# Attention scores of a two-branch streaming encoder: chunk mask written into PSUM by VectorE, score blocks joined and issued in one piece

## The chip, the cores and the metric

One core of one Trainium2 chip runs the whole program. The metric is the device time of one execution in microseconds; the time of a kernel is the median of its runs.

## The reference

Two layers of an encoder work on 320 tokens: 256 of a prompt and 64 of a second request (the sample), whose 256 earlier keys and values lie in a cache. Model width is 1024, everything is fp32. In a layer, one wide projection of the normed input feeds two branches, an attention branch and a gated linear attention (GLA) branch; the branches are projected, gated and merged, then a feed-forward layer and a per-layer input gate follow.

The change touches the attention branch alone. It has 8 heads; each head has two softmax maps (m = 0, 1) of 64 channels, and subtracts the second, times lambda, from the first:

```python
def diff_attend(q, k, v, lam, mask):
    s = jnp.einsum('bqhmd,bkhmd->bhmqk', q, k) * (A_DH ** -0.5)
    if mask is not None:
        s = jnp.where(mask, s, -jnp.inf)
    p = jax.nn.softmax(s, axis=-1)
    a = p[:, :, 0] - lam * p[:, :, 1]
    return jnp.einsum('bhqk,bkhe->bqhe', a, v)
...
        mask = k_chunk[None, :] <= q_chunk[:, None]
```

The mask is block-causal over chunks of 64 prompt tokens: a query sees the keys of its own chunk and of all earlier chunks. The sample attends to its cached and its own 64 keys without a mask.

## The kernel before

**Layout and stages.** Activations lie transposed in SBUF, 128 channels on the partitions and the 320 tokens along the free axis. Every projection is cut into tiles of 128 output channels. A tile is computed in 8 chunks of 128 input channels (k = 0 to 7), each with three matmuls, because weights and inputs are split into a high and a low part: lines 1201, 1202 and 1203 in `tile`. Its result grows in one of two PSUM banks, `big[0]` and `big[1]`. Weights come in by DMA (SP's queue, `w_raw`), ScalarE makes their high part (L559, `w_hi`), VectorE the low part (L843, `w_lo`), and PE waits for it at the head of a tile.

**The mix loop.** In each layer, the wide projection is run in 4 iterations of 16 tiles (`MIX_IT`, `MIX_N`), so that there are eight iterations in all. An iteration makes two attention heads and one GLA head. Its tiles are, in order: GLA queries and keys (0, 1), attention keys (2, 3), queries (4, 5), GLA values (6, 7), attention values (8, 9), and gates (10 to 15). The small matmuls of the two branches are issued by hand between the tiles or, through the generator argument `between` of `tile`, between the chunks of a tile: after each chunk, `tile` takes one step of the generator (L1206). Each engine has its own hand-written order of the same loop, and semaphores join them.

**The scores.** `scores(0)` (head 0 of the iteration) is stepped in tile 7 and `scores(1)` in tile 11. Its first two steps issue nothing. The third, after chunk k = 2, waits for the rotary result and the copied keys (head 0) or for the copied attention maps of head 0 (head 1), and issues the first matmuls. The scores go to PSUM: `X[4]` for map 0 and `X[5]` for map 1, with columns 0 to 255 for the second block of 128 queries (all 256 keys) and columns 256 to 383 for the first block (128 keys); `X[0]` for the sample (256 cached keys, then 64 own). For each block of queries:

- L1284: the keys that all queries of the block see (192 or 64 columns), one matmul per map; then a yield, so a chunk of the tile comes next;
- L1288: the last 64 keys, one matmul per map, left open for accumulation;
- L1290: one matmul per map with a contraction of one row, which adds -1e30 to the scores of the block's first 64 queries with these keys (`mq`, a row of the constants); then a yield.

The sample's scores (L1297, cached keys, a yield, own keys) close the piece, and the last one raises `scores_done`. In this way a head's scores spread over the chunks k = 2 to 7 of its tile. An fp32 matmul is shown as two records in the trace, an accumulating one of the tiles (fp32r) as one.

**What follows the scores.** On VectorE, `negmax` (L953) waits for `scores_done`, takes five row maxima (L956, L957, L958) and scales them (L960). In program order it stands in step t = 7 (head 0) and t = 11 (head 1), behind the weight split of that step and ahead of the copy of that tile's result. ScalarE's `exps` (L655) then makes the exponentials and, behind them, the next weight splits. VectorE's `difference` (L965 to L974) follows in step 8 (head 0) or 12 (head 1); behind head 0's stand the masked sums of the GLA branch (L1040, L1043). PE transposes the maps in `att_transposes` (L1305 to L1309) after tile 9 (head 0) and tile 13 (head 1). After tile 9 it first waits for the first masked sum (L1395), then transposes the GLA values (L1211).

**What stands behind tile 7 on PE.** After tile 7, PE waits for the decayed GLA queries and keys (`gla_qk_ready`), which VectorE makes in step t = 6 (L1021 to L1028, from `E`), transposes the keys (L1211) and multiplies pairs (L1392). After tile 11 come the GLA's own sums (L1328).

**Counting.** `Steps` counts the VectorE instructions of an iteration that raise `dve_mix` (19 before), so that a wait on all of them so far can be put anywhere.

Of the kernel before, what the change touches and what calls it, by code (L numbers as in the profile page):

```python
# [26 lines left out]
P = 128  # L27
# [6 lines left out]
HEADS, DH, DV = 8, 64, 128  # L34
GH, GDK, GDV, RANK = 4, 128, 256, 16
CH = 64
# [36 lines left out]
K_ID, K_ONE, K_EPS = 0, 128, 256  # L73
# [8 lines left out]
K_MQ = K_ID2 + 64  # L82
# [26 lines left out]
def snap(eng, value):  # L109

    return value if isinstance(value, int) else eng.snap(value)
# [19 lines left out]
def encoder(nc, A, O):  # L131
# [27 lines left out]
    def sb(name, shape, dt=F32, where=ctx):  # L159
        return where.enter_context(nc.sbuf_tensor(name, shape, dt))  # L160

    def sem(name):
        return ctx.enter_context(nc.semaphore(name))
# [8 lines left out]
    cst = sb("cst", [P, NCONST])  # L172
# [86 lines left out]
    X = [ctx.enter_context(nc.psum_tensor(f"X{i}", [P, 512], F32)) for i in range(6)]  # L259
# [111 lines left out]
    dve_pro, dve_mix = sem("dve_pro"), sem("dve_mix")  # L371
# [460 lines left out]
    def _(dve):  # L832
# [46 lines left out]
        for l in range(DEPTH):  # L879
# [36 lines left out]
            for j in range(MIX_IT):  # L916
                tb = snap(dve, l * TILES + j * MIX_N)
                rb = snap(dve, l * RESULTS + j * MIX_N)
                v = snap(dve, l * MIX_IT + j + 1)
                st = Steps(dve, dve_mix, v * 19 - 19, 19)  # L920

                def at(per, k):
                    return v * per + (k - per)
# [28 lines left out]

                def negmax(h):  # L953
                    dve.wait_ge(scores_done, at(2, h + 1))
                    for m in range(2):
                        nc.vector.tensor_reduce(mx[:, m:m + 1], X[4 + m][:, 2 * P:3 * P], AX.X, ALU.max)  # L956
                        nc.vector.tensor_reduce(mx[:, 2 + m:3 + m], X[4 + m][:, 0:2 * P], AX.X, ALU.max)  # L957
                    st.put(nc.vector.tensor_reduce(mx[:, 4:5], X[0][:, 0:PAST + TS], AX.X, ALU.max))  # L958
                    st.wait()
                    nc.vector.tensor_scalar(nb[:, :], mx[:, :], -DH ** -0.5, None, ALU.mult).then_inc(negmax_ready, 1)  # L960
# [20 lines left out]
                for t in range(MIX_N):  # L981
# [32 lines left out]
                    if t in (6, 7):  # L1014
                        if t == 7:
                            negmax(0)
                        out_tile(vgT[:, t - 6, :], t)
# [28 lines left out]
                    if t in (10, 11):  # L1046
                        if t == 10:
                            dve.wait_ge(vg_trans, 2 * v)
                        else:
                            negmax(1)  # L1050
                        out_tile(zr[:, t - 10, :], t)
# [57 lines left out]
            for j in range(OUT_IT):  # L1109
                tb = snap(dve, l * TILES + j * OUT_N + OUT_0)  # L1110
                for t in range(OUT_N):
                    lo(tb, t + 2, KC)
                    dve.wait_ge(tile_done, tb + (t + 1 + CREDIT_TILE))
                    m = j * 4 + t
# [26 lines left out]
            for j in range(FDN_IT):  # L1141
                tb = snap(dve, l * TILES + j * FDN_N + FDN_0)
                for t in range(FDN_N):
                    lo(tb, t + 2, FDN_K[(t + 2) // 2 % 3])
                    if t // 2 % 3 == 2:
                        dve.wait_ge(tile_done, tb + (t + 1 + CREDIT_TILE))
                        m = j * 4 + t // 6 * 2 + t % 2
# [7 lines left out]
            for j in range(PLE_IT):  # L1155
                tb = snap(dve, l * TILES + j * PLE_N + PLE_0)
                n8 = snap(dve, l * KC + j * PLE_N)
                for t in range(PLE_N):
# [9 lines left out]
                    m = j * 4 + t  # L1168
# [17 lines left out]
    def _(pe):  # L1186
        mm = nc.tensor.matmul
# [50 lines left out]
        for l in range(DEPTH):  # L1238
# [17 lines left out]
            for j in range(MIX_IT):  # L1256
                tb = snap(pe, l * TILES + j * MIX_N)
                rb = snap(pe, l * RESULTS + j * MIX_N)
                v = snap(pe, l * MIX_IT + j + 1)
                xc = snap(pe, l * 24)  # L1260

                def at(per, k):
                    return v * per + (k - per)

                def scores(h):


                    q, k, kc = qr[:, h, :], kr[:, h, :], kcT[:, h, :]
                    mq = cst[0:1, K_MQ:K_MQ + P]
                    yield  # L1270
                    yield
                    if h == 0:
                        pe.wait_ge(rope_ready, 2 * v)
                        pe.wait_ge(k_copied, at(7, 5))
                    else:
                        pe.wait_ge(att_copied, at(6, 3))

                    for at0, q0, nk in ((0, P, 2 * P), (2 * P, 0, P)):
                        for m in range(2):
                            r = slice(m * DH, (m + 1) * DH)
                            mm(X[4 + m][:, at0:at0 + nk - CH], q[r, q0:q0 + P], k[r, 0:nk - CH], start=True, stop=True)  # L1284
                        yield
                        for m in range(2):
                            r = slice(m * DH, (m + 1) * DH)
                            mm(X[4 + m][:, at0 + nk - CH:at0 + nk], q[r, q0:q0 + P], k[r, nk - CH:nk], start=True, stop=False)  # L1288
                        for m in range(2):
                            mm(X[4 + m][:, at0 + nk - CH:at0 + nk], mq, cst[0:1, K_ONE:K_ONE + CH], start=False, stop=True)  # L1290
                        yield
                    for at0, keys in ((0, kc), (PAST, k[:, TP:T])):
                        if at0:
                            yield
                        for m in range(2):
                            r = slice(m * DH, (m + 1) * DH)
                            last = mm(X[0][r, at0:at0 + (PAST if at0 == 0 else TS)], q[r, TP:T], keys[r, :], start=True, stop=True)  # L1297
                    last.then_inc(scores_done, 1)
# [54 lines left out]
                for t in range(MIX_N):  # L1353
                    pe.wait_ge(result_read, rb + (t - 1 + CREDIT_RES))
                    tile(tb, t, x_hi, x_lo, chunk_wait=(xlo_ready, xc) if t == 0 else None,
                         between={7: scores(0), 11: scores(1), 15: gla_outputs()}.get(t, ()))
                    if j == t == 0:
                        if l:
# [114 lines left out]
            with pe.Fori(0, FDN_IT) as j:  # L1473
                tb = snap(pe, l * TILES + j * FDN_N + FDN_0)
                for t in range(FDN_N):
                    pair, k, mt = t // 6, t // 2 % 3, t % 2
# [39 lines left out]
        for c in range(KC):  # L1516
            pe.wait_ge(y_ready, c + 1)
            half, m = c // 4, c % 4
# [81 lines left out]
```

## Time and profile before

| What | Value |
|---|---|
| Time, median of 3 runs | 1573.46 us (1572.07 to 1576.39) |
| The profiled execution's own time | 1574.4 us |
| Its span, first to last instruction | 1572.6 us |
| PE (TensorE matmul) busy | 1520.7 us, 97% of the span |
| PEld (its weight loads, beside PE) | 1418.0 us, 90% |
| DVE (VectorE) busy | 872.0 us, 55% |
| ACT (ScalarE) busy | 622.8 us, 40% |
| POOL (GpSimd) busy | 243.3 us, 15% |
| HBM traffic | 121 GB/s over the span |
| Mean granted TensorE clock | 0.956 of 2.4 GHz |

How to read it: busy times are the union of an engine's instructions. Matmuls are pipelined, so one lasts longer in the record than the distance to the next; what a piece of PE work costs is read from start to start. The eight iterations of the mix loop lie in 30 to 430 us and 800 to 1200 us of the span. An idle stretch of an engine is written in brackets behind the instruction that ends it, with what it waited for. The granted clock is 1.00 at 2.4 GHz and 0.50 at 1.2 GHz; the value of a window is its mean.

### The profile page before, as it was taken

How to read it: one execution, taken by the hardware profiler on the slowest of the kernel's cores; microseconds unless marked ns; L12 is line 12 of the kernel's file. 1: busy time of each engine (PE TensorE's matmuls, PEld its weight loads, DVE VectorE, ACT ScalarE, POOL GpSimd, SP SyncE). 2: the span in 40 equal slices, each digit the busy share in tenths (PEclk: the TensorE clock that was granted, in tenths of full speed). 3: DMA queues.
4: the chain of work that ended last, by engine and by line, in shares of the span. 5: the costliest groups of instructions: out<-in, count | busy, mean ns of one | idle time of the engine just before them, and what ended most of it. 6: DMA issues, size and time to landing. Idle time of an engine off the chain costs nothing.

```text
span 1572.6 us, 25415 instructions
## 1 busy us (share of the span) xinstructions
PE 1520.7 (97%) x10019; PEld 1418.0 (90%) x10019; DVE 872.0 (55%) x1408; ACT 622.8 (40%) x1037; POOL 243.3 (15%) x276
## 2 busy tenths in 40 slices
PE   6899999999999999999989999999999999999997
PEld 4789888898799999999978898988888999999997
DVE  4653636546466655545556366463654565555546
ACT  3343343433463444333343244343345443343343
POOL 0302103021002200012422030110300050000224
PEclk9998989989899999999989799898997999999999
DMA  6467855555234444444423665335431445444443
GB/s 157 109 86 90 108 111 124 80 112 108 81 120 150 147 147 150 152 155 139 143 85 111 111 99 89 95 114 114 110 113 62 152 134 160 149 145 153 156 141 101
DMA packets 195552, 191.29 MB, mean 122 GB/s; under 512 B 9126, under 2 KB 192236, under 8 KB 195468
## 3 DMA queue, kind: packets, MB, share of 16 engines
q1 hardware_dynamic: 192352, 181.76, 46.1%
q0 software_dynamic: 2688, 7.35, 1.2%
q8 instruction: 57, 0.93, 0.2%
q10 hardware_dynamic: 428, 1.03, 0.2%
q14 instruction: 27, 0.22, 0.0%
HBM read 181.45 MB, written 8.65 MB: 121 GB/s over the span
## 4 chain that ended last, share of the span: by engine, by line
PE 85%; POOL 5%; DVE 5%; DMA 2%; ACT 2%; issue 1%; ACTq 0%; DVEq 0%; SPq 0%; POOLq 0%
PE big L1201 24%; PE big L1202 21%; PE big L1203 21%; PE X L1346 2%; POOL E L527 2%; DMA w_raw<-in_w_in 2%; PE X L1392 2%; PE X L1345 2%; PE X L1328 1%; POOL E L528 1%; PE X L1290 1%; DVE w_lo L843 1%; PE X L1211 1%; POOL rot L534 1%; PE X L1297 1%
## 5 line engine op out<-in xcount | busy, mean ns | idle before, releaser
L1201 PE MATMUL big<-x_hi,w_hi 128*128 128x320 f32 x1984 | 656.8, 331 | 20.4 <-DVE x_lo L1092 6.9
L1202 PE MATMUL big<-x_lo,w_hi 128*128 128x320 f32 x1984 | 625.3, 315 | 0.0
L1203 PE MATMUL big<-x_hi,w_lo 128*128 128x320 f32 x1984 | 624.2, 315 | 0.0
L843 DVE TENSOR_TENSOR w_lo<-w_raw,w_hi 128x1024 fp32r<-128x1024 f32 (+1 forms) x330 | 418.6, 1271 | 109.9 <-ACT w_hi L559 109.5
L1201 PEld LDWEIGHTS big<-x_hi,w_hi 128*128 128x128 f32 x1984 | 382.7, 193 | 56.6 <-issue 38.1
L1202 PEld LDWEIGHTS big<-x_lo,w_hi 128*128 128x128 f32 x1984 | 384.6, 194 | 3.5 <-issue 1.6
L559 ACT CAST w_hi<-w_raw 128x1024 fp32r<-128x1024 f32 x328 | 331.1, 1038 | 142.5 <-PE big L1203 86.3
L1203 PEld LDWEIGHTS big<-x_hi,w_lo 128*128 128x128 f32 x1984 | 383.7, 193 | 0.0
L504 POOL TENSOR_TENSOR sqt<-xT 128x320 f32<-128x320 f32 x47 | 48.0, 1021 | 637.3 <-DVE xT L1149 422.6
L1201 PE MATMUL big<-h_hi,w_hi 128*128 128x320 f32 x352 | 109.1, 310 | 0.0
L1203 PE MATMUL big<-h_hi,w_lo 128*128 128x320 f32 x352 | 108.9, 309 | 0.0
L1202 PE MATMUL big<-h_lo,w_hi 128*128 128x320 f32 x352 | 108.9, 309 | 0.0
L655 ACT ACTIVATE p<-X,nb 128x128 f32<-128x128 f32 (+1 forms) x64 | 26.1, 420 | 162.3 <-DVE nb L960 162.3
L1073 DVE TENSOR_TENSOR gab<-big,rstd 128x320 f32<-128x320 f32 x32 | 15.7, 490 | 128.0 <-PE big L1203 127.8
L527 POOL TENSOR_TENSOR E<-E 128x160 f32<-128x160 f32 x48 | 39.9, 831 | 247.9 <-DVE E L944 247.9
L783 ACT CAST h_hi<-f3z 128x640 f32 (+1 forms) x22 | 16.1, 730 | 139.5 <-DVE f3z L1133 139.5
L506 POOL TENSOR_TENSOR ssq<-ssq,sqt 128x320 f32<-128x320 f32 x47 | 68.3, 1454 | 3.7
L1130 DVE TENSOR_TENSOR f3z<-big,rstd 128x320 f32<-128x320 f32 x44 | 21.6, 492 | 81.4 <-PE big L1203 81.4
L1201 PEld LDWEIGHTS big<-h_hi,w_hi 128*128 128x128 f32 x352 | 66.1, 188 | 0.1
L1202 PEld LDWEIGHTS big<-h_lo,w_hi 128*128 128x128 f32 x352 | 66.1, 188 | 0.0
L1203 PEld LDWEIGHTS big<-h_hi,w_lo 128*128 128x128 f32 x352 | 66.1, 188 | 0.0
L728 ACT ACTIVATE qr<-X 128x320 f32<-128x320 f32 x16 | 7.0, 438 | 108.8 <-PE X L1346 108.8
(227 smaller groups left out, 1900.5 us busy)
## 6 DMA issues: line engine op xcount, KB each, us to landing
w_raw<-in_w_in SPq DMA_DIRECT2D x130, 512.0 KB, 7.1
w_raw<-in_w_f SPq DMA_DIRECT2D x120, 512.0 KB, 4.3
w_raw<-in_w_pb SPq DMA_DIRECT2D x16, 512.0 KB, 4.4
w_raw<-in_w_pa SPq DMA_DIRECT2D x16, 512.0 KB, 4.0
w_raw<-in_w_o SPq DMA_DIRECT2D x16, 512.0 KB, 4.2
w_raw<-in_w_ple_gate SPq DMA_DIRECT2D x16, 512.0 KB, 4.4
w_raw<-in_w_f SPq DMA_DIRECT2D x16, 384.0 KB, 3.6
k_raw<-in_cache_k SPq DMA_DIRECT2D x8, 256.0 KB, 9.3
```

The costliest lines, as they stand in the source:

```text
L504: nc.gpsimd.tensor_tensor(sqt[:, None, :], xT[:, chunk, :], xT[:, chunk, :], ALU.mult).then_inc(pool_sq, 1)
L506: nc.gpsimd.tensor_tensor(ssq[:, :], ssq[:, :], sqt[:, :], ALU.add).then_inc(pool_acc if n[2] else ssq_ready, 1)
L527: nc.gpsimd.tensor_tensor(o1, ref, first, ALU.subtract).then_inc(args_ready, 1)
L559: nc.scalar.copy(w_hi[:, t % 4, 0:nk, :], w_raw[:, (t // 2) % 2, 0:nk, (t % 2) * P:(t % 2 + 1) * P]).then_inc(hi_ready, 1)
L655: nc.scalar.activation(dst, src, ACT.Exp, bias=nb[:, n:n + 1], scale=DH ** -0.5, accum_out=sums[:, n:n + 1]).then_inc(probs_ready, 1)
L843: tt(w_lo[:, t % 4, 0:nk, :], w_raw[:, (t // 2) % 2, 0:nk, (t % 2) * P:(t % 2 + 1) * P], w_hi[:, t % 4, 0:nk, :].bitcast(F32), ALU.subtrac ...
L1201: mm(out, wh, xh[:, k0 + k, :], start=start and k == 0, stop=False)
L1202: mm(out, wh, xl[:, k0 + k, :], start=False, stop=False)
L1203: last = mm(out, wl, xh[:, k0 + k, :], start=False, stop=stop and k == nk - 1)
L1345: mm(out, old, E[:, NL + 1, c * CH:(c + 1) * CH], start=True, stop=False)
L1346: last = mm(out, vg_tok[chunk_rows(c), c // 2, ec], a_sum[chunk_rows(c), c // 2, :], start=old is None, stop=True)
L1392: last = mm(X[1 + pair][chunk_rows(c), lev * CH:(lev + 1) * CH], lhs, rhs, start=True, stop=True)
```

## The change

The mask leaves PE. The two blocks of keys of each query block become one matmul per map (256 and 128 columns) that writes all scores, also those that the mask forbids. VectorE overwrites these with -1e30 in PSUM, for each map by one memset of 64 partitions x 2 x 64 columns, waits until they are written, and then takes the maxima as before. All yields between the pieces are gone: after chunk k = 2 the four prompt matmuls and the four sample matmuls are issued in a row, and the chunks k = 3 to 7 follow without a break.

```diff
-                st = Steps(dve, dve_mix, v * 19 - 19, 19)
+                st = Steps(dve, dve_mix, v * 23 - 23, 23)
...
                 def negmax(h):
                     dve.wait_ge(scores_done, at(2, h + 1))
+                    for m in range(2):
+
+                        ahead = X[4 + m][0:CH, 0:512].rearrange("p (a b) -> p a b", b=P)[:, 1:3, CH:P]
+                        st.put(nc.vector.memset(ahead, -1e30))
+                    st.wait()
                     for m in range(2):
...
-                    mq = cst[0:1, K_MQ:K_MQ + P]
...
                     for at0, q0, nk in ((0, P, 2 * P), (2 * P, 0, P)):
                         for m in range(2):
                             r = slice(m * DH, (m + 1) * DH)
-                            mm(X[4 + m][:, at0:at0 + nk - CH], q[r, q0:q0 + P], k[r, 0:nk - CH], start=True, stop=True)
-                        yield
-                        for m in range(2):
-                            r = slice(m * DH, (m + 1) * DH)
-                            mm(X[4 + m][:, at0 + nk - CH:at0 + nk], q[r, q0:q0 + P], k[r, nk - CH:nk], start=True, stop=False)
-                        for m in range(2):
-                            mm(X[4 + m][:, at0 + nk - CH:at0 + nk], mq, cst[0:1, K_ONE:K_ONE + CH], start=False, stop=True)
-                        yield
+                            mm(X[4 + m][:, at0:at0 + nk], q[r, q0:q0 + P], k[r, 0:nk], start=True, stop=True)
                     for at0, keys in ((0, kc), (PAST, k[:, TP:T])):
-                        if at0:
-                            yield
                         for m in range(2):
```

The row `mq` of the constants stays in its table and is still loaded with it.

## Rows read from the trace of the kernel before

**Rows 1.** The page: busy time by engine, and the chain that ended last.

```profile
PE 1520.7 (97%) x10019; PEld 1418.0 (90%) x10019; DVE 872.0 (55%) x1408; ACT 622.8 (40%) x1037; POOL 243.3 (15%) x276
...
PE 85%; POOL 5%; DVE 5%; DMA 2%; ACT 2%; issue 1%; ACTq 0%; DVEq 0%; SPq 0%; POOLq 0%
```

**Rows 2.** Groups on PE: line, tiles, stationary, moving, xrecords | busy us, mean ns | idle.

```profile
L1290 PE MATMUL X<-cst 1*128 1x64 f32 x128 | 21.4, 287 | 0.0
L1288 PE MATMUL X<-kr,qr 64*128 64x64 f32 x128 | 14.3, 301 | 0.0
...
L1284 PE MATMUL X<-kr,qr 64*128 64x192 f32 x64 | 9.5, 375 | 3.1 <-DVE qr L951 3.1
...
L1284 PE MATMUL X<-kr,qr 64*128 64x64 f32 x64 | 7.2, 302 | 0.0
```

**Rows 3.** Timeline of PE, tiles 10 and 11 of one iteration: start us, us.

```profile
960.02 0.31 PE L1201 MATMUL big<-x_hi,w_hi 128*128 128x320 f32 x1
...
960.46 0.31 PE L1201 MATMUL big<-x_hi,w_hi 128*128 128x320 f32 x1
...
964.73 0.60 PE L1284 MATMUL X<-kr,qr 64*128 64x192 f32 x4
965.25 0.41 PE L1201 MATMUL big<-x_hi,w_hi 128*128 128x320 f32 x1
...
965.88 0.44 PE L1288 MATMUL X<-kr,qr 64*128 64x64 f32 x4
966.25 0.65 PE L1290 MATMUL X<-cst 1*128 1x64 f32 x4
966.84 0.42 PE L1201 MATMUL big<-x_hi,w_hi 128*128 128x320 f32 x1
...
970.06 0.65 PE L1297 MATMUL X<-kcT,qr 64*64 64x256 f32 x4
970.64 0.41 PE L1201 MATMUL big<-x_hi,w_hi 128*128 128x320 f32 x1
...
971.27 0.33 PE L1297 MATMUL X<-kr,qr 64*64 64x64 f32 x4
971.53 0.70 PE L1328 MATMUL X<-vg_tok,kdT 64*128 64x256 f32 x2
```

**Rows 4.** Timeline of the same iteration: PE and DVE around its two heads.

```profile
938.86 0.60 PE L1284 MATMUL X<-kr,qr 64*128 64x192 f32 x4 [0.45 <-DVE qr L951]
...
940.25 0.16 DVE L1021 COPY ebl<-E 128x5 f32<-128x5 f32 x1
...
943.54 0.49 DVE L1028 TENSOR_TENSOR E<-E,qg 128x320 f32<-128x320 f32 x1
...
945.67 0.55 PE L1211 MATMUL X<-cst,E 128*128 128x128 f32 x3
945.78 0.29 DVE L956 TENSOR_REDUCE mx<-X 128x1 f32<-128x128 f32 x1 [0.61 <-PE X L1297]
...
954.82 0.96 DVE L1043 TENSOR_REDUCE a_sum<-a_msk 128x64 f32<-128x448 f32 x1
...
957.31 0.82 PE L1211 MATMUL X<-cst,vgT 128*128 128x128 f32 x6
...
971.65 0.29 DVE L956 TENSOR_REDUCE mx<-X 128x1 f32<-128x128 f32 x1 [7.09 <-PE X L1297]
```

**Rows 5.** Busy time and granted clock by window (columns in the first line).

```profile
core 0: us, PE busy (x) PEld busy (x) DVE busy (x) ACT busy (x) POOL busy (x), PEclk, DMA share, GB/s
169.30:176.20 6.90, 5.88 (x78) 4.91 (x77) 5.49 (x17) 1.73 (x9) 0.00 (x0) 1.00 0.81 132
262.05:271.74 9.69, 9.69 (x47) 6.73 (x47) 6.32 (x18) 0.00 (x0) 0.27 (x1) 0.65 0.54 123
290.80:299.02 8.22, 8.22 (x48) 5.55 (x47) 0.00 (x0) 0.00 (x0) 0.99 (x2) 0.80 0.86 116
964.73:976.21 11.48, 11.48 (x76) 9.13 (x76) 2.11 (x7) 2.77 (x11) 0.99 (x2) 1.00 0.76 152
864.55:880.57 16.02, 16.02 (x77) 12.46 (x77) 4.49 (x13) 5.62 (x15) 0.99 (x2) 0.68 0.47 114
```

## The prediction

> **What bounds the kernel now.** I read the page first. TensorE is busy 97% of the span and 85% of the chain that ended last is PE [rows 1], so a matmul that goes away is worth its time unless something else is due at that place just behind it. Everything the change touches lies in the eight iterations of the mix loop (two layers of four), each with a first head in tile 7 and a second head in tile 11: 16 score sections. The groups of instructions on PE give the size of the work [rows 2]: the mask line L1290 has 128 records, L1288 128, L1284 64 + 64. An fp32 matmul is two records, so a head has 8 mask records, 8 of L1288 and 8 of L1284, beside 8 of L1297 for the sample rows. The durations there are latencies of pipelined matmuls; what a piece costs is the distance from its start to the next piece's start, and that I read from the timeline of one second head [rows 3].
>
> **PE, one head, before** [rows 3]. 192-column piece 964.73 to 965.25: 0.52. Four 64-column records 965.88 to 966.25: 0.37. Four mask records 966.25 to 966.84: 0.59. The next block repeats the pattern with 64 columns in place of 192: 0.37, 0.37, 0.59. Sample keys 970.06 to 970.64: 0.58; own keys 971.27 to 971.53: 0.26. Sum 3.65 us. Between them lie five projection chunks of three matmuls (k = 3 to 7). A chunk among its like takes 960.46 - 960.02 = 0.44; between two score pieces it takes 0.63 (965.25 to 965.88; 970.64 to 971.27 the same), so entering and leaving a score piece costs 0.19. The section is 971.53 - 964.73 = 6.80 us.
>
> **PE, one head, after.** The masks are gone (-1.18). The two joined blocks are four records of 256 columns and four of 128. From 0.37 at 64 columns and 0.52 at 192, 0.0012 us a column gives 0.45 at 128 and 0.60 at 256 (the 256-column L1297 piece takes 0.58). With 0.58 and 0.26 for the sample rows: 1.89 us. One thing is new: the 64*128 matmuls are followed directly by the 64*64 ones of L1297, with no chunk between. No row shows that turn; it lies between 0 and the 0.19 of a full turn, I take 0.1. Of the chunks only k = 3 (entered from the piece) and k = 7 (followed by fp32 work) keep half a turn each: 5 x 0.44 + 0.19 = 2.39. The section becomes 1.89 + 0.10 + 2.39 = 4.4 us: **2.4 us of PE work saved per head**. The waits at the head of the piece (rotary result and key copy for head 0, the copied attention map for head 1) stand where the first piece stood before; no DMA moves with it, and SP's and POOL's queues issue nothing for it. The scores of a head are complete after 2 us instead of 6.8.
>
> **First heads: not all of it is path.** Behind tile 7, PE transposes the decayed keys, and these come from VectorE. In the iteration of [rows 4] the piece starts at 938.86 and the transposes at 945.67. VectorE's last decay product runs from 943.54 to 944.03; with 0.05 for the signal PE can go on at 944.08. The shortened section would be through at 943.26, so PE waits 0.8 us there, and the gain is 945.67 - 944.08 = **1.6 us**, not 2.4. What is late next is VectorE's products, an engine whose queue at that place the change does not shorten.
>
> **The added VectorE work.** Two memsets of 64 partitions x 128 elements in PSUM and a wait on their completion, ahead of the five reductions. No row has a memset. Bounds: 0.16 (a copy of 5 columns) and 0.49 (320 columns) [rows 4]; I take 0.29, the reduction over 128 PSUM columns, as nearest in size; two make 0.58, the wait included. By the Trainium skill (VectorE: DVE Perf Modes, "Zero memsets can be issued as uint32") a memset takes one cycle per element, so size and not dtype should set it; no run here shows that yet. For a first head: VectorE had waited 0.61 us for the scores before the first reduction at 945.78, so it is free at 945.17; the scores now are there, the memsets take until 945.75, and the reductions start as before. The chain behind (exponentials, difference, mask sums) is unmoved; its first mask sum ends at 955.78 and PE wants it behind tile 9, at 957.31 before, 955.7 after: the two meet. So the memsets are hidden by a wait that existed, with nothing to spare, and I count **1.5 us** for a first head. For a second head VectorE had waited 7.09 us [rows 4]; the scores come 4.8 us earlier in the section, and the section itself 1.5 us earlier, the memsets cost nothing on the path, and the whole 2.4 us count: the maps are asked for only two tiles later. The weight transfers hang on VectorE's weight splits in the tiles ahead and move with them.
>
> **The clock.** The windows by stage [rows 5] show three score sections in which the granted clock was not 1.00 (2.4 GHz) but partly 0.5 (1.2 GHz): a first head of 9.69 us at a mean of 0.65 (6.81 at full clock), a second of 8.22 at 0.80 (6.80), and a stretch of 16.02 us at 0.68 whose twin at 1.00 takes 11.48. They cost 2.88 + 1.42 + 4.54 = 8.8 us. What PE did before each fall was the scattered form: small pieces of half the rows, one-row masks, short chunks. After the change the dense chunks stand together. I expect these falls to go.
>
> In the second iteration PE already waited 1.0 us for the decayed keys (window of 6.90 us with PE busy 5.88) and the clock stayed at 1.00 [rows 5]. There a first head gains nothing, and the wait grows by 2.4 to 3.4 us. I charge a fall of the clock there at the cheapest seen, 1.4; its ends are 0 (as in that row) and 4.5.
>
> **Sum.** Seven first heads x 1.5 = 10.5; eight second heads x 2.4 = 19.2; clock 8.8; less 1.4: **37.1 us**. From the profiled execution's own 1574.4 us (span 1572.6): 1537.3. The median of the three runs, 1573.46, is 0.06% below the profiled one, so **1536.5 us**.
>
> **Rivals.**
> (B) The work goes but the clock is not recovered: falls move elsewhere, since the low stretches at the end of each iteration remain and everything shifts against them. Gain 10.5 + 19.2 = 29.7: 1544. For it: only 3 of 16 sections fell, so it is a matter of chance which do. Against: all three fell inside the scattered form.
> (C) VectorE is late in the first heads: memsets at 0.49 with the signal on top (1.1 us together) put reductions and mask sums 0.5 us later, PE waits behind tile 9 as well, or an engine behind eats the rest. With nothing left of the first heads: 37.1 - 10.5 = 26.6, 1547. For it: slack is nil there. Against: even at the upper end of the price 1.0 of the 1.5 us stays.
> (D) Slower: bunching the scores leaves PE idle for 0.8 us ahead of the key transposes of each first head, with small matmuls around it, and the granted clock falls to half there. Priced at the dearest fall, 4.54 us x 8 = 36.3 against 29.7 gained: 1574.4 + 6.6, about **1580**. It decides from seven such falls. Against it: the second iteration's wait of 1.0 us at the same place, with the clock at 1.00 [rows 5]. The Trainium skill (TensorE: Matmul & The Clock Gate, "HAM oscillation") states that waits between bursts of matmuls put the engine back to half clock, so that each burst starts slow. By that rule this one would come out on the slow side, as in D; the trace agrees that falls occur and are dear (0.68 mean, 4.54 us), but not that a gap of this size causes one.
> That the change does less than it says is no rival of weight: the masks are out of the program and the yields between the pieces are gone.
>
> **How the numbers follow.** Forecast 0.64, its own range 1528 to 1543 (the turn at 0 or 0.19 per head is +-1.6; second iteration 0 to 4.5; falls that come or go elsewhere a few us). B 0.20, C 0.10, D 0.04, and 0.02 for no change. The range takes in B and C: 1527 to 1549. A measurement of this kernel tells about 0.3% (4.7 us) from no change: faster by more 0.94, within 0.02, slower 0.04.
>
> **What would show it.** In the changed kernel: no mask records on PE and 8 records of joined blocks per head; a second-head section of 4.4 us; a first-head section of about 5.2 us that ends with PE waiting some 0.8 us for VectorE's decay product; two memsets of about 0.3 us ahead of the reductions; a second-head reduction that starts within 2.1 us of the piece; clock 1.00 in the three sections named. Wrong if the sections shrink but iterations don't (then a wait behind tile 9 or for weights has grown), if the clock falls behind the first heads (D), or if the section stays above 5 us at full clock, which would put the turns between matmul shapes above what I read.

## The result and the profile after

The changed kernel takes **1524.88 us** (median of 4 runs, 1522.66 to 1530.12) beside 1574.76 us for the kernel before (median of 4): a ratio of 0.969 [0.966, 0.9719], 49.9 us less. The forecast of 1536.5 us had the direction, but the time lies below the lower end of its range, 1527. The profiled execution took 1522.66 us with a span of 1520.9, against 1572.6: 51.7 us to account for.

The page of the changed kernel: busy time by engine, and the chain that ended last [rows 1].

```profile
PE 1459.1 (96%) x9763; PEld 1383.4 (91%) x9763; DVE 878.1 (58%) x1440; ACT 621.8 (41%) x1037; POOL 243.4 (16%) x276
...
PE 84%; DVE 7%; POOL 5%; DMA 2%; issue 1%; ACT 1%; ACTq 0%; DVEq 0%; SPq 0%; POOLq 0%
```

PE has 256 records fewer and 61.6 us less busy time; the span lost only 51.7, and VectorE's share of the chain rose from 5 to 7%. PE still sets the end. The groups of instructions on PE that make the scores [rows 2], and VectorE's new one (columns: line, engine, operation, tiles, shapes, xrecords | busy us, mean ns | idle before and its releaser):

```profile
L1288 PE MATMUL X<-kr,qr 64*128 64x256 f32 x64 | 11.2, 428 | 2.6 <-DVE qr L951 2.6
L1292 PE MATMUL X<-kcT,qr 64*64 64x256 f32 x64 | 10.4, 402 | 0.0
L1288 PE MATMUL X<-kr,qr 64*128 64x128 f32 x64 | 6.2, 270 | 0.0
L1292 PE MATMUL X<-kr,qr 64*64 64x64 f32 x64 | 4.5, 217 | 0.0
L958 DVE MEMSET X<- 64x128 f32 x32 | 4.9, 165 | 12.9 <-PE X L1292 12.7
```

The 128 mask records are gone, the joined blocks are 64 + 64 records, and VectorE has 32 memsets of 0.165 us. What a piece costs is again read from start to start. The timeline of a second head of the changed kernel, PE and DVE [rows 3]:

```profile
1020.46 0.92 PE L1288 MATMUL X<-kr,qr 64*128 64x256 f32 x8
1021.31 0.65 PE L1292 MATMUL X<-kcT,qr 64*64 64x256 f32 x4
1021.80 0.28 PE L1292 MATMUL X<-kr,qr 64*64 64x64 f32 x4
1022.01 0.41 PE L1206 MATMUL big<-x_hi,w_hi 128*128 128x320 f32 x1
...
1022.18 0.31 DVE L958 MEMSET X<- 64x128 f32 x2 [1.53 <-PE X L1292]
...
1022.52 0.29 DVE L961 TENSOR_REDUCE mx<-X 128x1 f32<-128x128 f32 x1
...
1024.40 0.48 PE L1323 MATMUL X<-vg_tok,kdT 64*128 64x256 f32 x1
```

The section lasts 1024.40 - 1020.46 = 3.94 us instead of 6.80, and the first reduction starts 2.06 us after the piece. Both blocks together take 0.85, the cached sample keys 0.49, the own ones 0.21: 1.55 us. The five chunks and their turns take the remaining 2.39.

A first head of the same kernel, PE and DVE [rows 4]:

```profile
996.17 0.92 PE L1288 MATMUL X<-kr,qr 64*128 64x256 f32 x8 [0.43 <-DVE qr L951]
...
1000.87 0.48 DVE L1033 TENSOR_TENSOR E<-E,qg 128x320 f32<-128x320 f32 x1
1001.27 1.21 DVE L843 TENSOR_TENSOR w_lo<-w_raw,w_hi 128x1024 fp32r<-128x1024 f32 x1
1001.40 0.55 PE L1216 MATMUL X<-cst,E 128*128 128x128 f32 x3 [1.22 <-DVE E L1033]
...
1002.50 0.31 DVE L958 MEMSET X<- 64x128 f32 x2
1002.84 0.29 DVE L961 TENSOR_REDUCE mx<-X 128x1 f32<-128x128 f32 x1
...
1011.87 0.96 DVE L1048 TENSOR_REDUCE a_sum<-a_msk 128x64 f32<-128x448 f32 x1
...
1013.04 0.82 PE L1216 MATMUL X<-cst,vgT 128*128 128x128 f32 x6
```

The section lasts 1001.40 - 996.17 = 5.23 us, and its end is VectorE's: PE waits 1.22 us for the last decay product. Five of the eight first heads are like this one; that of iteration 1 takes 3.84 us without a wait, that of iteration 5 takes 4.64, and the second iteration's is told below. The memsets start when VectorE's own weight split ends (1001.27 + 1.21 = 1002.48), so VectorE is late there and not waiting for scores.

With the same marks in all eight iterations (starts of the PE rows just named, then of the first GLA output matmul L1340/L1341, and of the two sums over `o_sq`) the spans of both kernels divide as follows. The GLA outputs are the small matmuls that stand between the chunks of tile 15.

| Stretch on PE, sum of eight, us | before | after | difference |
|---|---|---|---|
| first-head section | 58.48 | 44.62 | -13.9 |
| key transposes to second head's scores | 152.48 | 155.06 | +2.6 |
| second-head section | 57.48 | 31.52 | -26.0 |
| GLA own sums to GLA outputs | 133.88 | 131.26 | -2.6 |
| GLA outputs to the `o_sq` sum | 95.39 | 83.85 | -11.5 |
| that sum to the end of the iteration | 48.97 | 47.30 | -1.7 |
| all else (start, layer change, tail) | | | +1.4 |

Two stretches that the diff does not touch changed, at the ends of the iterations. Their windows in the changed kernel (columns in the first line), four of eight:

```profile
core 0: us, PE busy (x) PEld busy (x) DVE busy (x) ACT busy (x) POOL busy (x), PEclk, DMA share, GB/s
299.90:313.30 13.40, 13.40 (x77) 11.31 (x77) 5.02 (x7) 7.42 (x15) 1.09 (x2) 1.00 0.81 156
386.66:404.52 17.86, 17.86 (x77) 15.09 (x77) 3.05 (x5) 4.78 (x10) 0.00 (x0) 0.71 0.18 59
1040.78:1054.17 13.39, 13.39 (x77) 11.30 (x77) 3.40 (x6) 4.78 (x10) 1.10 (x2) 1.00 0.50 113
1127.53:1145.36 17.83, 17.83 (x78) 15.04 (x77) 3.05 (x5) 4.79 (x10) 0.00 (x0) 0.71 0.20 60
```

and in the kernel before, the two kinds that it has (one of 19.36, seven of 17.85 to 17.87):

```profile
213.93:233.29 19.36, 19.36 (x77) 16.49 (x77) 3.04 (x5) 4.79 (x10) 0.00 (x0) 0.65 0.41 94
987.90:1005.75 17.85, 17.85 (x77) 15.07 (x77) 3.05 (x5) 4.79 (x10) 0.00 (x0) 0.71 0.34 111
```

PE is busy for the whole of every such window, with the same 77 records; only the granted clock differs. At 1.00 the work takes 13.4 us. Before, part of it ran at half clock in all eight iterations; after, iterations 3 and 7 kept full clock, and iterations 2 and 6 took 15.00 and 16.43. That is 13.2 us of the gain. What stands ahead of such a stretch does not tell which kind it will be: iterations 3, 4, 6, 7 and 8 of the changed kernel are alike on PE to 0.02 us in all four stretches ahead of it (5.23, 19.06, 3.94 and 16.38 us at full clock), and their output windows took 13.40, 17.86, 16.43, 13.39 and 17.83.

The second iteration went the other way. PE and ScalarE there, in the changed kernel's timeline:

```profile
163.07 1.99 ACT L559 CAST w_hi<-w_raw 128x1024 fp32r<-128x1024 f32 x2 [8.49 <-DMA w_raw<-in_w_in]
...
169.52 0.90 PE L1216 MATMUL X<-cst,E 128*128 128x128 f32 x3 [5.96 <-DVE E L1033]
```

and in the kernel before:

```profile
165.23 2.00 ACT L559 CAST w_hi<-w_raw 128x1024 fp32r<-128x1024 f32 x2 [6.40 <-DMA w_raw<-in_w_in]
...
171.69 0.55 PE L1211 MATMUL X<-cst,E 128*128 128x128 f32 x3 [1.02 <-DVE E L1028]
```

In the changed kernel the first-head section starts at 159.55, 4.2 us earlier than before (163.79), while the weights that ScalarE splits come by DMA and are late: ScalarE's split, which waits for them, starts at 163.07 against 165.23 in the kernel before, only 2.2 us earlier. PE waits 5.96 us at the key transposes for VectorE's product; the clock falls to half near the end of this wait (a mean of 0.96 over the section), and the stretch behind takes 21.71 us instead of 19.06, 6.1 of them at half clock.

### The profile page after: what moved, and what is told of

It is laid out like the page before. It is cut to its first block, busy times and chain, and to the rows that moved or that the text cites. A ratio compares the mean times of both kernels' runs of the same rounds, so it can differ in the third digit from the quotient of the medians.

```text
span 1520.9 us, 24935 instructions
## 1 busy us (share of the span) xinstructions
PE 1459.1 (96%) x9763; PEld 1383.4 (91%) x9763; DVE 878.1 (58%) x1440; ACT 621.8 (41%) x1037; POOL 243.4 (16%) x276
## 4 chain that ended last, share of the span: by engine, by line
PE 84%; DVE 7%; POOL 5%; DMA 2%; issue 1%; ACT 1%; ACTq 0%; DVEq 0%; SPq 0%; POOLq 0%
PE big L1206 23%; PE big L1207 22%; PE big L1208 22%; PE X L1341 2%; POOL E L527 2%; PE X L1387 2%; PE X L1340 2%; DVE w_lo L843 2%; PE X L1323 1%; DMA w_raw<-in_w_in 1%; POOL E L528 1%; PE X L1492 1%; PE X L1216 1%; POOL rot L534 1%; PE X L1304 1%
## 5 line engine op out<-in xcount | busy, mean ns | idle before, releaser
L1206 PE MATMUL big<-x_hi,w_hi 128*128 128x320 f32 x1984 | 645.9, 326 | 18.4 <-DVE x_lo L1097 6.9
L589 ACT ACTIVATE x_hi<-xT,cur 128x320 fp32r<-128x320 f32 x48 | 26.2, 560 | 52.4 <-DVE xT L1121 31.5
```

Of the source, the lines that this page charges most:

```text
L589: nc.scalar.activation(x_hi[:, m, :], xT[:, m, :], ACT.Copy, scale=cur[:, col + m:col + m + 1]).then_inc(xhi_ready, 1)
L1206: mm(out, wh, xh[:, k0 + k, :], start=start and k == 0, stop=False)
```

## Experiments

Two things had to be separated: the work on PE from the clock, and the masks from the bunching. The theory: the work at full clock is the same in every iteration, the score sections fall because of the masks, and which output stretch falls goes with the time at which it comes. The rivals: bunching or scattering as such moves the clock in the score sections, and the output stretches fall less because of what the score sections ahead of them no longer do. All kernels ran beside the kernel before, with medians of 1570.47 and 1570.34 us on the two chips used.

**1. The mask moved alone.** Pieces and yields stay as before.

```diff
-  mm(X[4 + m][:, at0 + nk - CH:at0 + nk], q[r, q0:q0 + P], k[r, nk - CH:nk], start=True, stop=False)
-  for m in range(2):
-      mm(X[4 + m][:, at0 + nk - CH:at0 + nk], mq, cst[0:1, K_ONE:K_ONE + CH], start=False, stop=True)
+  mm(X[4 + m][:, at0 + nk - CH:at0 + nk], q[r, q0:q0 + P], k[r, nk - CH:nk], start=True, stop=True)
...
+  (two memsets and the wait, as in the change)
```

> The kernel before, with only the mask moved: two memsets in negmax, no one-row matmuls; blocks and pieces stay as they were between the chunks. Work theory: each head loses its two mask pieces of 0.58, so a second-head section goes from 6.80 to 5.6 us; a first head would be through at 938.86 + 5.64 = 944.5, just behind VectorE's 944.08, so it gains the same 1.2. 16 x 1.2 = 19 us: 1556. Whether the clock still falls in the scattered score sections is open: with the three falls gone (8.8 us) 1547. Rival (one piece, not the mask, is what counts): less than 8 us gained.

Measured: 1552.83 us, ratio 0.9891 [0.9865, 0.9917]. A second-head section of this kernel, by window:

```profile
945.91:951.55 5.64, 5.64 (x40) 3.80 (x40) 0.00 (x0) 0.00 (x0) 0.98 (x2) 1.00 1.03 109
```

5.64 instead of 6.80: the eight mask records cost 1.16 us a head, where the start-to-start distances of [rows 3] gave 1.18. No score section ran below full clock; only behind the second iteration's first head, with its wait, did it fall (20.55 us at a mean of 0.92 where 19.06 is usual). So the scattered form by itself does not bring the clock down in a score section. The time lies between the two expected, 1556 and 1547: the falls in the score sections are gone, but the second iteration gives back 2.7 us and the output windows 1.6 (146.0 us in sum against 144.3). Score sections without falls did not spare the output windows.

**2. One piece alone.** Masks and split blocks stay; the yields between them go.

```diff
-                        yield
                         for m in range(2):
...
-                        yield
                     for at0, keys in ((0, kc), (PAST, k[:, TP:T])):
-                        if at0:
-                            yield
```

> The kernel before, with only the yields between the score pieces removed: masks stay on PE, blocks stay split, all score matmuls of a head stand in one piece. Work theory: five turns of 0.19 become one and the pieces lose their leaving cost; section 6.8 to about 5.5, 1.3 us a head, 1554 at full clock. Clock theory: 3 us of small and one-row matmuls in a row make the granted clock fall behind most heads; at 1.4 to 3 us each for 16 heads 1575 to 1600, slower than before. If the clock holds in all sections, the masks were not what made it fall in the scattered form.

Measured: 1555.26 us, ratio 0.9904 [0.9875, 0.9933]. Two score sections, by window, a first head and the second head of the same iteration:

```profile
926.32:933.27 6.95, 6.95 (x48) 6.40 (x49) 6.95 (x21) 0.00 (x0) 0.27 (x1) 0.75 0.59 131
952.27:957.80 5.53, 5.53 (x48) 4.85 (x47) 1.72 (x6) 0.48 (x3) 0.98 (x2) 1.00 1.00 153
```

At full clock a section is 5.53 us, but 5 of the 16 ran at a mean of 0.75 or 0.76 and took 6.95 to 7.07 (first heads 3, 5, 6 and 7, second head 1). Bunching with the masks in did not make the clock fall everywhere, which a time of 1575 to 1600 would have meant, nor did it stop the falls. The output windows take 147.4 us in sum, 3.0 more than before.

**3. Joined blocks without masks, but spread** over the chunks, the four pieces behind k = 2, 4, 6 and 7 (against the changed kernel).

```diff
                             mm(X[4 + m][:, at0:at0 + nk], q[r, q0:q0 + P], k[r, 0:nk], start=True, stop=True)
+                        yield
+                        yield
                     for at0, keys in ((0, kc), (PAST, k[:, TP:T])):
+                        if at0:
+                            yield
```

> The changed kernel, but the four score pieces of a head stand between chunks again (after k = 2, 4, 6 and 7). Work theory: three more turns of 0.19: second-head section 3.94 to 4.5, first heads still end at VectorE's decay product (5.2), so 8 x 0.57 = 4.6 us slower than the changed kernel: 1529.5, plus or minus the falls of the clock at the ends of the iterations, which shift. Rival (one piece is what brings most): 1545 or more.

Measured: 1532.91 us, ratio 0.9763 [0.9738, 0.9789]; a second-head section of 4.68 us, a first-head section of 5.23 as in the changed kernel in five iterations, and no score section below full clock but the one with the wait. A second head, timeline of PE (each piece, and what starts behind it):

```profile
1028.52 0.70 PE L1288 MATMUL X<-kr,qr 64*128 64x256 f32 x4
1029.15 0.41 PE L1206 MATMUL big<-x_hi,w_hi 128*128 128x320 f32 x1
...
1030.22 0.49 PE L1288 MATMUL X<-kr,qr 64*128 64x128 f32 x4
1030.65 0.42 PE L1206 MATMUL big<-x_hi,w_hi 128*128 128x320 f32 x1
...
1031.72 0.65 PE L1296 MATMUL X<-kcT,qr 64*64 64x256 f32 x4
1032.30 0.41 PE L1206 MATMUL big<-x_hi,w_hi 128*128 128x320 f32 x1
...
1032.93 0.33 PE L1296 MATMUL X<-kr,qr 64*64 64x64 f32 x4
1033.20 0.48 PE L1327 MATMUL X<-vg_tok,kdT 64*128 64x256 f32 x1
```

With chunks between them the four pieces cost 0.63, 0.43, 0.58 and 0.27 by these rows, 1.90 us in sum before rounding; in a row the same matmuls cost 1.55. Putting the four pieces together is therefore worth 4.68 - 3.94 = 0.74 us in a second head (three turns fewer, 0.25 each) and nothing in the five first heads where VectorE's product ends the section either way (0.84 in that of iteration 1). Its span is 10.0 us longer than the changed kernel's: 5.9 of these lie in the second heads, another 5.9 in the output stretches (137.0 us in sum against 131.2), and the rest takes 1.8 back.

**4. The kernel before with dense work ahead of the outputs.** Twelve matmuls of the ordinary kind open tile 12 and write into a bank that the tile's first chunk starts afresh; score code and output code are untouched.

```diff
+            for _ in range(pad):
+                mm(out, w_hi[:, t % 4, 0, :], xh[:, k0, :], start=True, stop=True)
             for k in range(nk):
...
-                         between={7: scores(0), 11: scores(1), 15: gla_outputs()}.get(t, ()))
+                         between={7: scores(0), 11: scores(1), 15: gla_outputs()}.get(t, ()), pad=12 if t == 12 else 0)
```

> The kernel before, with 12 more dense matmuls at the head of tile 12 in each iteration (the first one of the tile repeated, each overwritten by the next): 12 x 0.147 = 1.76 us, 14.1 us over eight iterations. The score code is that of before. Timing theory (the clock's falls in the GLA outputs of tile 15 depend on when that stretch comes, not on what the scores look like): some of the eight output stretches, all 11.6 to 12.5 us before, come near 8.6 us, and the time rises by clearly less than 14 us or varies from run to run. Rival (the denser scores are what keeps the clock up at the end of the iteration): all eight stretches stay at 11.6 to 12.5 us and the time is 1574.8 + 14.1 = 1589.

Measured: 1589.40 us (1581.91 to 1596.59), ratio 1.0123 [1.0077, 1.017]. One output window of this kernel:

```profile
216.95:233.32 16.37, 16.37 (x78) 13.77 (x78) 3.05 (x5) 4.79 (x10) 0.00 (x0) 0.79 0.41 84
```

Six of its eight output windows take 16.37 to 16.41 us, the length of none in the kernel before; their sum is 134.2 against 144.3 us. So these stretches change with unchanged score code, by a shift of 1.76 us an iteration, though none comes near full clock, as the timing theory had expected of some. The median is close to what the rival gives, and 18.9 us above the kernel before beside it. In the profile (of the run of 1584.13 us) this does not come about as the rival has it: 10.2 us are won in the output windows and 6.3 lost in and behind the score sections, of which five now fell (first heads 3, 4, 6 and 7, second head 5).

**5. The changed kernel with the GLA outputs spread.** Their four parts, which stood behind four successive chunks of tile 15, are stepped over tiles 14 and 15, one behind every third chunk, and the `o_sq` sum directly behind the last.

```diff
+                def spaced(parts):
+                    while True:
+                        yield
+                        yield
+                        next(parts, None)
+                        yield
...
-                         between={7: scores(0), 11: scores(1), 15: gla_outputs()}.get(t, ()))
+                         between={7: scores(0), 11: scores(1), 14: outputs, 15: outputs}.get(t, ()))
```

> The changed kernel, with the four GLA output parts stepped over the chunks of tiles 14 and 15, three chunks apart, in place of behind the first four chunks of tile 15. Same matmuls. Clock theory: the output stretch is where the granted clock falls in nearly all iterations, because small weight-heavy matmuls stand close together; with dense chunks between, the clock holds at 1.00 in all eight. The trace of the changed kernel has two iterations without a fall, 8.6 + 4.8 us; all eight like them would be 107 against 131 us: 24 us less, about 1501. Rival (the falls there are a matter of the iteration's timing alone, whatever stands in it): clock still falls in several iterations, 1515 to 1525.

Measured: **1497.39 us**, ratio 0.952 [0.9483, 0.9556], the fastest kernel here. An output window of it, which holds 19 more records than those above because more chunks lie between the parts:

```profile
1019.79:1035.84 16.05, 16.05 (x96) 13.95 (x96) 5.02 (x7) 7.12 (x15) 1.09 (x2) 1.00 0.58 134
```

All eight are at 1.00. The stretch from the GLA's own sums to the iterations' end falls from 262.4 to 239.4 us in sum: the falls that the change had left there were worth 23 us. The output matmuls are the same; what is different is how much dense work lies between the parts. The rival, 1515 to 1525, is out.

**6. The same spreading in the kernel before.**

> The kernel before, with the same spreading of the GLA output parts and the score code as it was. Clock theory: output stretches without falls, 107 against 144 us: 37 us less, 1537 (a few us more or less for falls in the score sections, which stay). Against e5 it gives the price of the score change with no falls at the ends of the iterations: work theory 36 to 40 us (section sums 58.5 + 57.5 against 44.6 + 31.5 us, less 2.7 behind the second iteration's first head). Rival (the surplus of the change over its forecast came from the scores): the two stay 50 us apart as before.

Measured: 1549.13 us (1544.38 to 1561.14, 6 runs), ratio 0.984 [0.9799, 0.988], 12 us above what was expected. All output windows are at 1.00 here too, but the score sections, masks included, now fall oftener. A first head and a second head, by window:

```profile
350.31:360.04 9.73, 9.73 (x48) 6.78 (x48) 6.31 (x18) 0.00 (x0) 0.27 (x1) 0.65 0.53 113
949.33:957.76 8.43, 8.43 (x49) 5.71 (x48) 0.00 (x0) 0.00 (x0) 0.99 (x2) 0.77 0.92 167
```

Eight fell (first heads 4 and 8, second heads 3 to 8) instead of three. This profile is of the slowest of the six runs, 1561.14 us: its span is 62.2 us longer than that of experiment 5, and of these 30.0 are the lower clock in and behind the score sections, the other 32 the work at full clock. Between the medians of experiments 5 and 6 lie 51.7 us, as the rival had it, and not 36 to 40. The output windows of the two are alike, so the surplus over the work is the clock at the score sections that keep their masks in the profile, and by estimate some 20 us of it in the median run (51.7 less 32), which has no profile.

**7. More VectorE work ahead of the reductions.** Three pairs of memsets instead of one.

```diff
-                    for m in range(2):
-
+                    for m in (0, 1, 0, 1, 0, 1):
+                        if m == 0:
+                            st.wait()
```

> The changed kernel with each pair of memsets written three times, each round waiting for the one before: 0.7 us more of VectorE per head. Cover theory: in first heads the mask sums end 0.2 us before PE wants them behind tile 9, so all but 0.2 shows: 0.5 us in each of seven first heads, the stretch from the key transposes to the second head's scores goes from 19.06 to 19.5, 3 to 4 us in all, 1528; second heads pay nothing. Rival (VectorE's memsets are wholly covered): 19.06 unchanged. Rival (they are on the path of both heads): 11 us more, 1536.

Measured: 1536.87 us, ratio 0.9775 [0.9737, 0.9813]. Behind a first head, by window: key transposes to the second head's scores, first in this kernel, then in the changed one.

```profile
262.95:282.67 19.72, 19.28 (x175) 18.15 (x175) 15.87 (x34) 9.22 (x27) 0.28 (x1) 1.00 0.35 68
```

```profile
260.54:279.59 19.05, 19.05 (x175) 18.19 (x176) 15.39 (x30) 9.18 (x27) 0.28 (x1) 1.00 0.36 70
```

Four more memsets at 0.17 are 0.68 us, and 0.67 of it shows, 0.44 as idle PE. The slack behind a first head is indeed nil. Second heads stay at 3.94, so the rival with both heads on the path is out, although its 1536 is what was measured. Of the 12.4 us of longer span only 4.3 stand behind the first heads; 9.0 are in output windows that fell (140.2 us in sum against 131.2), and the first section starts 0.9 earlier. PE's instructions are those of the changed kernel; 0.67 us an iteration of later PE work was enough to change which output windows fall.

**8. The changed kernel with 16 dense matmuls an iteration**, placed as in experiment 4.

> The changed kernel with 16 more dense matmuls at the head of tile 12 in each iteration, 2.35 us, 18.8 us over eight. Timing theory: falls of the clock at the ends of the iterations move, so the output stretches of the eight iterations have another pattern than in the changed kernel (two of eight without a fall) and the total lies within 10 us of 1524.9 + 18.8 = 1543.7 on either side. Rival (the changed kernel's pattern belongs to its scores): again the third and the seventh iteration without a fall, 1543.7.

Measured: 1548.05 us, ratio 0.9851 [0.9811, 0.9891]. The matmuls themselves take 2.34 us an iteration (18.72 against 16.38), 18.7 in sum. Two output windows:

```profile
216.18:229.57 13.39, 13.39 (x77) 11.30 (x77) 3.14 (x5) 4.79 (x10) 0.00 (x0) 1.00 0.55 112
305.30:323.17 17.87, 17.87 (x77) 15.15 (x77) 4.88 (x7) 6.29 (x14) 1.09 (x2) 0.71 0.45 95
```

Now iterations 2 and 5 keep full clock, and iterations 3 and 7, which kept it in the changed kernel, do not. Which stretch falls goes with when it comes, as experiment 7 has it without any change on PE; with the outputs this close together, neither the score code nor the output code decides it alone.

**Over all profiles.** Leaving out the second iteration's first head with its wait, 21 of 60 score sections fell in the four kernels that have the masks on PE (3 before, 5, 5 and 8 in experiments 2, 4 and 6), and none of 90 in the six that have not, be the pieces scattered, spread or together. What it is in the masks that does it (the single row, or eight more small records) no run separates. The eight output windows take 131.2 to 147.4 us in sum in the eight kernels that keep the outputs where they were; the changed kernel has the least of all.

## Why the prediction was wrong, point by point

**What held.** The two wait points were as forecast: the first-head section measured 5.23 us (forecast "about 5.2") with VectorE's decay product as its end, and behind it "nothing to spare", which experiment 7 shows to within 0.02 us. The first reduction of a second head came 2.06 us after the piece (forecast within 2.1). The falls of the clock in the score sections are gone, 2.9 + 1.4 + 1.6 us there and 2.9 behind one: 8.8, as counted. The prediction put the reason to the scattered form as a whole ("small pieces of half the rows, one-row masks, short chunks"); experiments 1 to 3 put it to the masks in it.

**First failed step: the price of the piece.** The prediction took "1.89 us" for the matmuls and "0.1" for the turn between the two kinds; it measured 1.55 for both. Its prices had been read from pieces that stand between chunks, and for such pieces they are right: experiment 3, where the same four pieces stand apart, gives 1.90. In these start-to-start distances a piece's turns are inside. In a row both blocks cost 0.85 and not 1.05, the cached keys 0.49 and not 0.58, the own ones 0.21 and not 0.26. The turn between the two forms is no less than one to a chunk: in the trace's single records the last 128-column pair is followed after 0.20 us, where its like was after 0.10, and the first pair of the cached keys after 0.26, where its like was after 0.21, both as in experiment 3. It stands inside the 1.55, so the 0.1 on top counted it twice. The chunks came out at the forecast 2.39. So the saving is 2.86 to 2.87 us in a second head, not 2.4: 22.9 us in eight, 3.7 more than the term (8 x 2.4). The seven first heads gave 13.1 instead of 10.5, since those of iterations 1 and 5 gained 2.97 and 2.19, with less wait for VectorE than in the one read.

**Second failed step: the low stretches at the iterations' ends.** The prediction named them only in rival B, as a place to which falls move, and in the range as "a few us". It showed no row of them and gave them no term. They held falls in eight of eight iterations, some 37 us over the 8 x 13.4 at full clock. The change took away 13.2 us of that, the largest error in the sum and the one that put the time below the range: without it the time would have been some 1538 us. Experiments 4, 7 and 8 show that a shift moves these stretches, with the score code unchanged or the masks gone: by -10.2 us against the kernel before, by +9.0 and +7.4 against the changed kernel. That the shift of this change went the good way is luck as far as the runs show: experiments 1 and 2 moved the same stretches by +1.6 and +3.0.

**Second iteration.** Forecast a loss of 1.4; measured 2.1 in the section and 2.6 behind it, 4.7 in all, 0.2 above the upper end given (0 to 4.5). The wait grew from 1.0 to 5.96 us, by 4.9 and not "by 2.4 to 3.4 us": 2.86 for the shorter section, and 2.08 because PE arrives 4.2 us earlier and the split behind the late DMA only 2.2.

**The sum, term by term**: 13.1 + 22.9 + 8.8 - 4.7 + 13.2 - 0.3 (the first iteration's stretch from the GLA's own sums, 16.63 against 16.37) - 1.4 (the first section starts that much later in this run, unexplained) = 51.6 of the 51.7 us; forecast 10.5 + 19.2 + 8.8 - 1.4 = 37.1. Apart from the 13.2, the errors nearly cancel (+2.6, +3.7, -3.3, -0.3, -1.4), which is luck too.

**The rivals.** B had the opposite sign of what the clock did. C is out: two memsets and the wait take 0.34 us (1022.18 to 1022.52), not 0.58 or 1.1, and the stretch behind a first head stays at 19.06. The Trainium skill (VectorE: DVE Perf Modes, "Zero memsets can be issued as uint32") has a cost that goes by elements; only one size ran here, so that rule was not tried. D is out: PE waits 1.22 us ahead of the key transposes and the clock stays at 1.00 behind it. Near the end of the 5.96 us of the second iteration it did fall, as the rule of the Trainium skill (TensorE: Matmul & The Clock Gate, "HAM oscillation") on waits between bursts has it; the falls that cost most here are not of that kind, as the windows with PE busy throughout show.

**What stays open.** Why one output stretch falls and its like in the next iteration does not is not settled: the runs say only that it goes with timing. Nor is it shown that this is why single runs of one kernel differ by some 15 us (experiments 4 and 6), since only one run of each has a profile. And which property of the masks brings the falls in the score sections is open.

## What to carry to other kernels

When scattered pieces are put together, price each from a row in which a like piece follows it, or take the turns out of the start-to-start distance; adding turns to distances that hold them counts them twice. Look at the granted clock of every stretch, also of those the diff leaves alone: where they are low, any shift can move them, here from 13.2 us less to 3.0 us more than before, and the range must hold that. And once such stretches are found, they are worth a change of their own: the same small matmuls with more dense chunks between the parts took another 27.5 us off this kernel (1524.88 to 1497.39; 23.7 by the profiled spans).

## What was not expected of the hardware

The clock fell without PE having been idle. In the changed kernel's last iteration (timeline of PE) the pitch of the small output matmuls (two records) goes from 0.36 to 0.62 us, and that of a chunk's first matmul from 0.26 to 0.43, in the middle of an unbroken row of work:

```profile
1128.98 0.43 PE L1341 MATMUL X<-a_sum,vg_tok 64*128 64x64 f32 x2
1129.34 0.42 PE L1206 MATMUL big<-x_hi,w_hi 128*128 128x320 f32 x1
1129.60 0.31 PE L1207 MATMUL big<-x_lo,w_hi 128*128 128x320 f32 x1
...
1131.06 0.44 PE L1340 MATMUL X<-E,s_past 128*128 128x64 f32 x2
1131.43 0.69 PE L1341 MATMUL X<-a_sum,vg_tok 64*128 64x64 f32 x2
1132.05 0.63 PE L1206 MATMUL big<-x_hi,w_hi 128*128 128x320 f32 x1
1132.48 0.47 PE L1207 MATMUL big<-x_lo,w_hi 128*128 128x320 f32 x1
```

Ahead of the fall stand two parts of the outputs with one dense chunk between them; with the parts further apart (experiment 5) no such window fell in eight iterations. And the one-row mask matmuls cost more than their own time: beside 1.16 us a head at full clock stand falls in 21 of 60 sections, where sections without them had none in 90.
